# The last period of a mixture-of-experts layer: the down projection of item 30 goes in front of the gate/up product of item 31, two tiles' bias sums into the wait for the last activation, and the bias rows are loaded sooner

## What is computed

```python
def moe(h, router_w, router_b, w_gu, b_gu, w_down, b_down):
    logits = (h @ router_w + router_b).astype(jnp.float32)
    top_vals, top_idx = lax.top_k(logits, TOP_K)            # 4 of 32 experts
    gates = jax.nn.softmax(top_vals, axis=-1)
    ...
    def expert_block(args):
        xb, e = args
        gu = xb @ w_gu[e] + b_gu[e]                         # 1024 -> 2048
        gate, up = jnp.split(gu, 2, axis=-1)
        gate = jnp.minimum(gate, SWIGLU_LIMIT)
        up = jnp.clip(up, -SWIGLU_LIMIT, SWIGLU_LIMIT)
        glu = gate * jax.nn.sigmoid(SWIGLU_ALPHA * gate)
        return ((up + 1.0) * glu) @ w_down[e] + b_down[e]   # 1024 -> 1024
    ...                                                     # gated, summed over each token's 4 experts
x = x + g2 * moe(h2)
return rms_norm(x, final_g)
```

## Time and profile before

| what | value |
|---|---|
| median of 3 runs | 1435.39 us (1434.9 to 1436.96) |
| the profiled execution | 1437.4 us |
| its span, from the first instruction to the last | 1435.5 us |
| TensorE busy, share of the span | 1319.4 us, 92% |
| VectorE, ScalarE, GpSimd busy | 58%, 51%, 25% |
| granted TensorE clock, mean over the span | 0.981 |
| moved by DMA | 475.90 MB, mean 332 GB/s |

### The profile page before, as it was taken

One profiled execution on the slowest core, in us unless ns is written; L12 is line 12 of the kernel. 1 busy time (PEld: TensorE's weight loads), 2 busy tenths in 40 slices (PEclk: granted clock), 3 DMA queues, 4 the chain that ended last, 5 costly groups with the idle time before them and its releaser, 6 DMA issues.

```text
span 1435.5 us, 17803 instructions
## 1 busy us (share of the span) xinstructions
PE 1319.4 (92%) x6418; PEld 864.3 (60%) x6423; DVE 839.3 (58%) x947; ACT 725.8 (51%) x940; POOL 355.8 (25%) x318
## 2 busy tenths in 40 slices
PE   3999999999999998998898998989899898998886
PEld 1767884557767555766473774746477556757432
DVE  0576676447947546758182783645576637748224
ACT  3542325546756636637273674544565627637212
POOL 3000020112123142413242332323233142414210
PEclk9999999999999999999999999999999999999998
DMA  9746640057899999999999999999999999999984
GB/s 342 246 149 221 226 175 16 9 184 277 329 379 410 413 409 410 402 390 392 397 392 403 379 401 390 374 402 378 401 391 390 382 388 384 402 375 377 401 332 142
DMA packets 95128, 475.90 MB, mean 332 GB/s; under 512 B 23686, under 2 KB 33902, under 8 KB 42816
## 3 DMA queue, kind: packets, MB, share of 16 engines
q1 hardware_dynamic: 82656, 451.39, 79.9%
q0 software_dynamic: 12304, 23.22, 5.9%
q10 hardware_dynamic: 80, 0.13, 0.0%
HBM read 468.16 MB, written 23.09 MB: 342 GB/s over the span
## 4 chain that ended last, share of the span: by engine, by line
PE 62%; DMA 23%; ACT 9%; DVE 4%; issue 1%; SPq 0%; DVEq 0%; ACTq 0%
DMA chunk<-in_w_down 21%; PE bank L1743 9%; PE bank L1746 9%; PE bank L1750 9%; PE bank L1792 4%; PE bank L1527 4%; ACT e_hi L921 3%; PE bank L1339 3%; ACT area L924 3%; PE bank L1822 3%; PE bank L1341 3%; PE bank L1340 3%; PE bank L1777 2%; PE bank L1814 2%; PE bank L1815 2%; DVE chunk_lo L2000 2%
## 5 line engine op out<-in xcount | busy, mean ns | idle before, releaser
L2000 DVE TENSOR_TENSOR chunk_lo<-chunk,e_hi 128x2048 fp32r<-128x2048 f32 x216 | 484.7, 2286 | 235.0 <-ACT e_hi L921 234.9
L921 ACT ACTIVATE e_hi<-chunk 128x2048 fp32r<-128x2048 f32 x216 | 407.8, 1913 | 282.6 <-DMA chunk<-in_w_down 219.4
L1777 PE MATMUL bank<-chunk,area 128*64 128x512 f32 x896 | 204.1, 608 | 26.1 <-DMA chunk<-in_w_gu 26.1
L1743 PE MATMUL bank<-e_hi,x_hi 128*128 128x512 f32 x576 | 226.7, 394 | 0.0
L1746 PE MATMUL bank<-e_hi,x_lo 128*128 128x512 f32 x576 | 224.3, 389 | 0.0
L851 POOL COPY future<-routes 128x1 int32 (+1 forms) x31 | 116.1, 3745 | 386.8 <-DVE area L2336 267.6
L1814 PE MATMUL bank<-e_hi,act_hi 128*128 128x512 f32 x288 | 121.1, 420 | 41.4 <-ACT e_hi L921 41.3
L1777 PEld LDWEIGHTS bank<-chunk,area 128*64 128x64 f32 x896 | 62.0, 138 | 157.5 <-issue 110.3
L1750 PE MATMUL bank<-chunk_lo,x_hi 128*128 128x512 f32 x576 | 154.0, 389 | 0.0
L1743 PEld LDWEIGHTS bank<-e_hi,x_hi 128*128 128x128 f32 x576 | 108.1, 188 | 26.1 <-issue 4.1
L1750 PEld LDWEIGHTS bank<-chunk_lo,x_hi 128*128 128x128 f32 x576 | 108.1, 188 | 22.5
(11 more groups left out here) (296 smaller groups left out, 1713.8 us busy)
## 6 DMA issues: line engine op xcount, KB each, us to landing
chunk<-in_w_gu SPq DMA_DIRECT2D x256, 1024.0 KB, 23.6
chunk<-in_w_down SPq DMA_DIRECT2D x128, 1024.0 KB, 24.3
ring<-in_ada_w SPq DMA_DIRECT2D x24, 1024.0 KB, 9.4
ring<-in_w_in SPq DMA_DIRECT2D x9, 1024.0 KB, 8.1
ring<-in_w_o SPq DMA_DIRECT2D x4, 1024.0 KB, 6.3
xs<-in_x SPq DMA_DIRECT2D x4, 512.0 KB, 5.0
ring<-in_w_in SPq DMA_DIRECT2D x8, 256.0 KB, 5.6
xn_rows<-area POOLq DMA_DIRECT2D x4, 512.0 KB, 5.9
```

What stands on the lines that cost most here:

```text
L921: return nc.scalar.activation(dst, src, ACT.Copy, scale=scale)
L1743: pe.matmul(bank[b][:], x_hi[:, c, :], hi, start=False, stop=False)
L1777: mm = pe.matmul(bank[g // 2][half, :], xgT[:, c, 0:NARROW], w[:, 512 * g:512 * g + 512], start=False, stop=(c == GU - 1))
L2000: tt(chunk_lo[period.raw_slot(c)][:], raw(period.raw_slot(c)), e_hi[:, c % PARTS, :].bitcast(F32), ALU.subtract).then_inc(lo_ready, 1)
```

## The change

In the last period the 4 down chunks of item 30 are loaded and multiplied before the 8 gate/up chunks of item 31 (`last_chunks`, `last_steady`, and `last_mixed` on ScalarE). Places 0 to 3 are now down of item 30, 4 to 11 gate/up of item 31, 12 to 15 down of item 31 as before. `gate_turn` moves into item 30's down product and to bank 5. The bias rows get a buffer of their own (in the place of `x_lo`, which the last wide item was the last to use) and are loaded in front of place 0. The four bias sums of tiles 0 and 1 run after the last gate/up chunk, ahead of the turning of item 31's activation, which now goes into one bank and is copied in one piece. After the `If` three bias sums remain ahead of the rows, (2,0), (3,1) and (2,1), and one, (3,0), ahead of tile 3's rows. The one-hot matrix, too, has a place of its own, and VectorE makes it and the gate sums before item 30's rows.

```diff
-        one_hot, ys_last = view(17408, T, P), uc
+        ys_last = uc
...
+        one_hot = nc.alloc_sbuf_tensor_at("one_hot", [P, T, P], F32, offset=-(-nc.sbuf_base // 32) * 32 + 2048)[:]
         x_hi = sb("x_hi", [P, KD, P], F32R)
+        b_rows = nc.alloc_sbuf_tensor_at("b_rows", [P, D], F32, offset=-(-nc.sbuf_base // 32) * 32)[:]
...
-        b_rows = ring[:, 4 * SLOT:4 * SLOT + D]
...
+            def down_bias():
+
+                for t in range(T):
+                    sp.dma_start(b_rows[32 * t:32 * t + 32, :].rearrange("e (g n) -> e g n", g=4),
+                                 b_rows_dram.rearrange("g e n -> e g n")).then_inc(b_rows_in, 16)
+
+            def last_chunks(i, e, e_before):
+
+                period = Later(i)
+                for q in range(DN):
+                    raw_free(period, q)
+                    if q == 0:
+                        sp.wait_ge(b_rows_stored, 16)
+                        down_bias()
+                    down_chunk(period, q, q, e_before)
+                for c in range(GU):
+                    raw_free(period, DN + c)
+                    s = period.raw_slot(DN + c)
+                    sp.dma_start(raw(s), w_gu[e, c * P:(c + 1) * P, :]).then_inc(raw_in[s], 16)
...
-            closing(E, e_before)
-            sp.wait_ge(b_rows_stored, 16)
+            last_chunks(E - 1, e, e_before)
+            closing(E, e)
...
-            sp.wait_ge(chunk_used, CHUNKS * (E - 1) + 1)
-            for t in range(T):
-                sp.dma_start(b_rows[32 * t:32 * t + 32, :].rearrange("e (g n) -> e g n", g=4),
-                             b_rows_dram.rearrange("g e n -> e g n")).then_inc(b_rows_in, 16)
+                down_bias()
...
+            def last_mixed():
+
+                period = Later(E - 1)
+                act_parts(E - 1)
+                a.wait_ge(chunk_used, period.at(DN))
+                copy(upper[0:NARROW, :], bank[4][NARROW:P, :]).then_inc(upper_moved, 1)
+                a.wait_ge(gate_t_full, 1)
+                copy(gate_t, bank[5][:, 0:P]).then_inc(gate_t_ready, 1)
+                glu(E - 1, period.at(CHUNKS))
+                a.wait_ge(at_full, 2 * E)
+                copy(last_actT[:], bank[6].rearrange("p (k n) -> p k n", k=4)).then_inc(ahi_ready, 2)
...
-            def last_act_turn():
-
-                pe.wait_ge(act_ready, E)
+            def bias_sum(t, half, first=True):
+
+                rows = slice(32 * t, 32 * t + 32)
+                return pe.matmul(bank[SUM_BANKS[t] + half][:], gate_t[rows, :],
+                                 b_rows[rows, half * 512:half * 512 + 512], start=first, stop=not first)
+
+            def first_bias_sums(loads):
+
+                pe.wait_ge(gate_t_ready, 1)
+                pe.wait_ge(y_ready, E)
+                pe.wait_ge(b_rows_in, 64 * loads)
                 for half in range(2):
-                    turned_taken(E - 1, half)
-                    turn_narrow(half)
+                    bias_sum(0, half)
+                    bias_sum(1, half)
...
             def last_steady():
                 period = Later(E - 1)
                 pe.wait_ge(act_ready, E - 1)
                 act_turn(E - 1, 0)
                 act_turn(E - 1, 1)
-                gate_up_narrow(period)
-                down(period, GU, last_act_turn)
+                down(period, 0, gate_turn)
+                gate_up_narrow(period, DN)
+                first_bias_sums(1)
+                pe.wait_ge(act_ready, E)
+                for half in range(2):
+                    turned_taken(E - 1, half)
+                    turn_narrow(half, bank[6])
...
-            down_narrow(Later(E), 0, bank[0], last_actT, gate_turn)
+            down_narrow(Later(E), 0, bank[0], last_actT)
             with pe.If(n_over > 0):
...
-            pe.wait_ge(gate_t_ready, 1)
-            pe.wait_ge(b_rows_in, 64)
-            pe.wait_ge(y_ready, E)
...
-            for half in range(2):
-                for t in range(T - 1):
-                    bias_sum(t, half)
+            bias_sum(2, 0)
+            bias_sum(3, 1)
+            bias_sum(2, 1)
             pe.wait_ge(rows_left, 1)
...
             bias_sum(T - 1, 0)
-            bias_sum(T - 1, 1)
             last_rows(T - 1)
...
             gate_sums()
             last_one_hot()
+            rows_out(E - 1, Later(E - 1).at(DN))
+            clip(E - 1, Later(E - 1).at(CHUNKS))
+            swiglu(E - 1)
             last_rows_out()
```

More of the change, by code:

```diff
@@ L103 @@
 NARROW = 64
-assert len(ORDER) == E and ORDER[:2] == "HH" and ORDER[-1] == "L"
+assert len(ORDER) == E and ORDER[:2] == "HH" and ORDER[-2:] == "LL"
 N_WIDE = ORDER.count("H")
@@ L658, in _ @@
             e_before, e = 0, 1
-            for i in range(1, E):
+            for i in range(1, E - 1):
                 gate_up_chunks(i, e)
@@ L663, in _ @@
                     sp.wait_ge(tables_ready, 1)
-                if i + 1 < E:
-                    e_next = sp.value_load(expert_at[0:1, i + 1:i + 2], min_val=0, max_val=E - 1)
-                    up_bias(i + 1, e_next)
+                e_next = sp.value_load(expert_at[0:1, i + 1:i + 2], min_val=0, max_val=E - 1)
+                up_bias(i + 1, e_next)
                 if i > 1:
@@ L1207, in mixed @@
                 glu(i, period.at(GU))
-                if i + 1 < E:
-                    x_parts(i + 1)
+                x_parts(i + 1)
                 if wide(i - 1):
@@ L1212, in mixed @@
                         hi(period, c)
-                if i + 1 < E and wide(i + 1):
+                if wide(i + 1):
                     for c in range(PARTS):
                         hi(after, c)
-                if i + 1 == E:
-                    for half in range(2):
-                        a.wait_ge(at_full, 2 * E + (half - 1))
-                        copy(last_actT[:, 2 * half:2 * half + 2, :],
-                             bank[6 + half][:, 0:256].rearrange("p (k n) -> p k n", k=2)).then_inc(ahi_ready, 1)
                 upper_rows(i)
@@ L1235, in _ @@
             a.wait_ge(tables_ready, 1)
-            for i in range(1, E):
+            for i in range(1, E - 1):
                 mixed(i)
             n_over = a.value_load(over_i[0:1, 16:17], min_val=0, max_val=OVER)
-            a.wait_ge(gate_t_full, 1)
-            copy(gate_t, bank[6][:, 0:P]).then_inc(gate_t_ready, 1)
+            last_mixed()
             a.wait_ge(chunk_used, MAIN_CHUNKS)
@@ L1700, in x_turn, with turn_narrow @@
                 mm.then_inc(xt_full, 1)
-            def turn_narrow(half):
+            def turn_narrow(half, out=None):
                 pairs = act[:, 0:512].rearrange("p (q f k) -> p q k f", q=2, k=2)
                 for k in range(2):
-                    mm = pe.transpose(bank[6 + half][:, k * P:(k + 1) * P], pairs[:, half, k, :], ident[:])
+                    o = bank[6 + half] if out is None else out[:, 256 * half:256 * half + 256]
+                    mm = pe.transpose(o[:, k * P:(k + 1) * P], pairs[:, half, k, :], ident[:])
                 mm.then_inc(at_full, 1)
@@ L1757, in gate_up, with gate_up_narrow @@
                         act_turn(1, 1)
-            def gate_up_narrow(period):
+            def gate_up_narrow(period, c0=0):
                 i = period.i
@@ L1772, in gate_up_narrow @@
                 for c in range(GU):
-                    pe.wait_ge(*period.landed(c))
-                    w = raw(period.raw_slot(c))
+                    pe.wait_ge(*period.landed(c0 + c))
+                    w = raw(period.raw_slot(c0 + c))
                     for g in range(4):
@@ L1829, in gate_turn @@
                 pe.wait_ge(gate_of_ready, 1)
-                pe.transpose(bank[6][:, 0:P], gate_rows, ident[:]).then_inc(gate_t_full, 1)
+                pe.transpose(bank[5][:, 0:P], gate_rows, ident[:]).then_inc(gate_t_full, 1)
             def opening(i):
@@ L1864, in steady, with end_first_bias_sums @@
                 down(period, GU)
-            def last_act_turn():
-                pe.wait_ge(act_ready, E)
-                for half in range(2):
-                    turned_taken(E - 1, half)
-                    turn_narrow(half)
+            def bias_sum(t, half, first=True):
[6 more added lines that the diff above has]
+                pe.wait_ge(b_rows_in, 64 * loads)
+                for half in range(2):
+                    bias_sum(0, half)
+                    bias_sum(1, half)
+            def end_first_bias_sums():
+                for half in range(2):
+                    bias_sum(0, half, False)
+                    bias_sum(1, half, False)
             def last_steady():
@@ L1895, in _ @@
             last_steady()
-            down_narrow(Later(E), 0, bank[0], last_actT, gate_turn)
+            down_narrow(Later(E), 0, bank[0], last_actT)
             with pe.If(n_over > 0):
+                end_first_bias_sums()
                 pe.wait_ge(gathered, E * 16)
-                pe.wait_ge(gate_t_ready, 1)
                 for half in range(2):
@@ L1908, in _ @@
```

(9 more changed lines are left out.)

## The result

The changed kernel takes 1441.96 us (median of 15 runs) against 1434.93 for the kernel before in the same session: a ratio of 1.0043, 95% interval 1.0034 to 1.0053. It is slower by 0.43%, which lies above the 0.2% that a measurement can tell, and outside the predicted range. One of the 15 runs of the kernel before took 6432.8 us; the ratio is of the fast runs and leaves it out. The profiled execution took 1443.33 us, its span 1441.5.

What follows compares the result with a forecast made beforehand. The weight stream's last chunk, waiting on one late DMA engine, then TensorE's branch, was taken to bound the end. Landing +1.9 less 0.1 behind the branch gave +1.8: 1437.2 us, range 1434.9 to 1439.2.

Steps and rivals of the forecast that it cites:

- TensorE's branch again near 3.6 us: Expected sign at the `If`: branch as long as before (3.593 us), bias sums starting 3.8 us after the last chunk's landing.
- the late fetch: Rival, chance 0.24: earlier scatter releases `xs` loads ahead of the branch's instruction packet; 1438.6 with one ahead, 1440.0 with two.
- Its price: In the late-fetch rival, each 512 KB `xs` load standing ahead of the instruction packet costs about 1.4 us.
- The rival of the clock: Half clock in tile 0's rows behind the branch goes away: -1.7 us, giving 1435.5; chance 0.11.
- The landing: Last weight chunk of period 31 lands 1.9 us later, about 1413.8; bounds -2.6 and +2.3.
- bias rows 1.4: Four 128 KB loads, now ahead of the last chunk on the late DMA engine, delay it 1.2 to 1.5 us.
- scatter 0.5: Item 30's scatter, now ahead of more chunks, delays the last chunk between nothing and 0.9 us; middle taken.
- the time SyncE takes to issue the bias rows does not show: About 11 us of issuing on a full queue, covered by the late engine's 30 us in line.
- The pause for the last activation: Period 31: 12.3 us from chunk twelve's landing to TensorE's end; sticks out at most 0.6, hidden under the branch; cost 0.
- The bias sums: Behind the branch, three remaining sums still take 2.04 us; priced by number, 1.0 would go.
- The order of the products: Period 31: same 12 chunks; 0.6 us later start, 0.3 for turned gates, covered by waits for data; cost 0.
- The tail: After the rows: one sum fewer saves TensorE 0.95 on tile 3, but VectorE without pause leaves 0.1 gained.

Runs made afterwards that it cites:

- e1: The changed kernel with the loads of the sums into `xs` held until VectorE has made the last rows: 1439.13 us, ratio 1.0034.
- e2: The kernel before with four more 512 KB loads, read by nobody, issued just ahead of the branch: 1439.43 us, ratio 1.0039.
- e5: The kernel before with only the bias rows moved, to a buffer of their own and loaded in front of period 31: 1435.42 us, ratio 1.0006.
- e4: The changed kernel with the last three bias sums in front of the `If` instead of behind it: 1438.27 us, ratio 1.0029.
- e6: The changed kernel with the last three bias sums in front of the `If` and the bias rows loaded in front of period 2: 1433.65 us, ratio 1.0000.
- e3: The changed kernel's product order and early scatter, but bias rows loaded behind all chunks and all bias sums behind the branch: 1439.81 us, ratio 1.0034.
- e7: The kernel of e6 with the sums loaded into free ring places, some 9 us ahead of the branch: 1432.82 us, ratio 0.9995.
- e9: The kernel of e7 unchanged, timed in more rounds: 1431.61 us, ratio 0.9989.
- before_again: The kernel before, unchanged, profiled a second time: 1434.89 us (one run).

## Why the prediction was wrong, point by point

**The step that failed** is "TensorE's branch again near 3.6 us". It took 5.85 and 5.80; the late fetch stood only as a rival, with 0.24. The forecast was 1.8 us in all and the loss 7.0; of the 5.2 between them 2.3 are the branch, 1.4 the landing and 1.5 what follows the branch. The rival's mechanism is the right one, and e1 and e2 show it from both sides: with the loads away the branch is short in the changed kernel, with loads added it is long in the old one. By loads issued just ahead the branch goes 3.4 to 3.7 (none, eight traces), 5.7 to 5.9 (two or three), 7.42 (four). The Trainium skill ("Runtime: NRT & Kernel Launch", Instruction fetch mechanics) says that the sequencer has its instructions fetched in blocks of 16 KiB over a DMA queue of its own; the one packet of 0.02 MB on the instruction queue agrees, and what the traces add is that a queue of its own does not bring the packet past loads that were issued ahead of it. The skill's figure for a compare-and-branch ("Advanced Engine Details and Errata", Control Flow Timing: about 108 ns) is far from TensorE's branch at the `If` in every trace here, 3.37 to 7.42 us; the measurement decides.

That the loads would be ahead could have been worked out from rows at hand. The prediction had the scatter done by about 1400, so only the third last chunk's use was left to release them. With the pause, the last four chunks run in one piece, so that use comes two chunks, 3.5 us, before TensorE's last matmul (1416.85 - 3.5 = 1413.3; SyncE issued at 1413.53), while the branch begins with the last landing, 2.6 us before it. SyncE needs 0.4 to 0.5 us a load, so two go ahead. The condition that the rival named was therefore met by the forecast's own numbers, and its chance should have been the larger.

**Its price** was 1.4 us for each load, 2.8 for two, against 2.2 to 2.3 measured, 2.3 for three in e2 and 3.8 for four: about 1 each. What the price left out is what goes with a longer pause. The rival of the clock was thought of as a gain only; here the half clock doubled, and 1.0 of the last 1.4 us is the bias sums' 2.99 where before they took 2.04. Long pauses and half clock go together in front of the rows: with pauses of 0.33 to 1.06 us there is none, with 1.30 to 1.98 us there is 3.41 us of it in three traces and none in one (e5, 1.62), with 3.31 to 5.67 us there is 6.83. But pauses of 1.99 to 2.63 us ahead of one of the last three gate/up chunks were followed by half clock in two traces (e4, e6) and by none in six. That the pause alone brings it is not shown.

**The landing** was put at +1.9 (bias rows 1.4, scatter 0.5, bound 2.3), and the term of the bias rows was too small. The five traces with bias rows and new order are at 73.5 to 75.3, mean 74.3, so +3.1. The four with the new order and the early scatter but without bias rows in front (e3, e6, e7, e9) are at 70.2 to 71.8, where the three of the old order without them (before, before_again, e2) are at 70.0 to 71.2: order and scatter cost nothing that these traces can tell, where 0.5 was put, and the bias rows cost all of the 3.1. In the old order, in the one trace of e5, they cost 1.3 to 2.5. Whether the order makes that difference stays open, and so does the reason for 3.1 instead of 1.4: no row here shows the sixteen engines one by one. One step of the prediction was not tried by itself, that the time SyncE takes to issue the bias rows does not show. The last chunk's load is issued 44.8 to 46.4 us after the bias matmul in the five traces and 42.1 to 43.1 in the four. But in e5 it is issued at 45.5 and lands at 72.5, so a late issue alone does not make the 3.1.

**The pause for the last activation** came out as worked out: 12.41 us from the landing of chunk twelve to TensorE's end (12.3), 0.6 past the landing-bound end (0.6), hidden under the branch. **The bias sums**: three products cost what six did, 1.98 us at full clock in e1 (2.0); the 2.99 of the changed kernel is the clock. **The order of the products** and VectorE's moved work: nothing in the chain waits for them. **The tail**: from tile 1's addition on VectorE has no pause, as foreseen.

What stays open besides: the right-hand columns of the table are of one execution each. 4 of the 15 times of the changed kernel lie at 1435.4 to 1437.0, the other 11 at 1440 to 1444, and both traces belong to the latter. Whether in those four the fetch left ahead of the loads, as it did by 0.26 us in e6, no trace shows.

## What to carry to other kernels

A branch that has to fetch its target is a small transfer with a deadline: when a change lets a wait end sooner, look at what that wait was holding back, and whether it now goes ahead of the fetch. Put such loads either well before the branch or behind its start, and put independent matmuls in front of the `If`, where they run while the fetch does. And take more than one trace before a term of a microsecond is called right: the landing moved by 1.2 us between executions of one stream, and the bias rows' 1.4 us, which the single trace of e5 seemed to bear out, were 3.1 in five traces of the new order.

## What the runs showed of the hardware

The branch of TensorE at the `If` took between 3.37 and 7.42 us, longer with more loads of 512 KB issued just ahead of it; loads issued 0.26 us behind its start did not lengthen it (3.42). The instruction packet began 1.0 to 1.2 us after the branch's start with none ahead and 5.0 us after it with four, and the branch ended 2.3 to 2.7 us behind the packet's beginning. With the longest pauses that it left (3.31 us and more) went 1.2 GHz for 6.83 us, in which, in e2, twelve passes of bias sums took 3.79 us instead of 2.04. And four loads of 128 KB, issued some 61 to 73 us ahead of the last landing, moved that landing by about 3 us in the new order of the products, and by 1.3 to 2.5 in the one trace of the old order.
